# A two-layer hybrid backbone: three weight buffers in the branch merge, and decays beside rates on the two halves of the array

## The chip, the cores and the metric

One core of one Trainium2 chip runs the whole program. The metric is device time in microseconds of one execution; the profile's own span goes from the first to the last instruction.

## The reference

Two layers (DEPTH = 2) over 256 context tokens and 512 latent tokens, D_MODEL = 1024. In each layer a norm, one wide projection, three parallel branches of width 512 (short convolution, bidirectional RWKV-7 scan, neighbourhood attention), the merge of the branches, an output product, and a SwiGLU FFN. The change touches two places. The first is the preparation of the scan's inputs, for two directions:

```python
    for d, offset in enumerate((1, -1)):
        zd = z + mu[d] * (shift_seq(z, offset) - z)
        r, k, v, lw, la = jnp.split(zd, RWKV_SPLITS, axis=-1)
        w_log = -jax.nn.softplus(-(w0[d] + jnp.tanh(lw) @ w2[d])) - 0.5
        decay = jnp.exp(-jnp.exp(w_log.astype(f32)))
        a = jax.nn.sigmoid(a0[d] + la @ a2[d])
```

The second is the merge:

```python
def merge_branches(gate_u, branches, w_up, w_o):
    gates = jax.nn.sigmoid(gate_u.reshape(gate_u.shape[:-1] + (N_BRANCH, D_MODEL)))
    proj = jnp.einsum('btnm,nmd->btnd', jnp.stack(branches, axis=-2), w_up)
    return jnp.sum(gates * proj, axis=-2) @ w_o
```

In the second layer the context tokens are no output, so its merge works on 512 of the 768 tokens.

## The kernel before

Channels lie on partitions and tokens on the free axis, in two segments: s = 0 is the context (256 columns), s = 1 the latent tokens (512 columns). Each large product is split in three: weights and activations are each a rounded part and a rest, and `split_products` (L279 to L281) issues high x high, high x low, low x high. ScalarE rounds a weight slab (ACT), GpSimd subtracts to make its rest (POOL), TensorE multiplies (PE). SyncE issues the loads (SP), in one queue and in program order. Each engine runs its own instructions in order; semaphores (`Count`) join them. The drain that GpSimd makes behind each rest hands the slab's slot back to SyncE.

**Scan stages.** For each of HP = 4 head pairs and each direction d, the weights `SMALL` hold w2 in rows 0 to 63 and a2 in rows 64 to 127, and `LD` holds tanh(lw) and la on the same rows. `decay_and_rate(d)` (L998) makes four plain f32 products: decay ("w") of segment 1 into PSUM bank 7, of segment 0 into bank 6, then rate ("a") the same way. A product waits until ScalarE or VectorE has emptied its bank (`at_bank.free`). ScalarE's sigmoids (L1172) empty them, between two activation table loads (L1163, L1174). There are 16 such groups: 4 in the two prologues ("pro", head pair 0, no scan blocks around them) and 12 in the body stages, where a filler deals these products and the products of the wide projection out between the scan's small block products, in proportion to costs (`COST`, `prep`). The whole order is written out when the kernel is built.

**Merge.** Eight output tiles of 128 channels, two a pass, four passes (the first is written out, the other three are a loop). A pass has six steps, u = 0 to 5: branch n = u % 3 of tile b = u // 3. Each step multiplies one up-weight slab of KM = 4 blocks; its rounded part and rest lie in one of two buffers (`W_HI[u % 2]`, `W_LO[u % 2]`), so ScalarE rounds the slab of step u when the product of step u - 2 is done. The gates of tile b (three branches in one load, L2278) get one sigmoid (L2292), in the loop behind the rounding of that tile's first slab. VectorE multiplies product and gate (L2354), adds (L2360) and splits the sum (L2364, L2366). A product's two banks come round every four steps. SyncE loads the three slabs of a tile and then its gates. Ahead of the first pass GpSimd also loads the residual again (L2329), after the rests of steps 0 and 1.

## Time and profile before

| | us |
|---|---|
| median of 3 runs | 3557.06 (3556.63 to 3567.53) |
| the profiled execution | 3564.53 |
| its span | 3562.8 |

The profile is that of one execution. "Busy" is the time in which an engine has an instruction of the program under way; a figure in brackets behind a timeline row is the engine's idle time just before it, with what ended it. A window row gives its stretch and length, then busy time and records of TensorE's matmuls (PE), its weight loads (PEld), VectorE (DVE), ScalarE (ACT) and GpSimd (POOL), then the granted TensorE clock, the DMA engines' busy share and GB/s. Every plain f32 product leaves two matmul records, every rounded one a single record.

### The profile page before, as it was taken

The numbers are of one execution on the slowest core, as the hardware profiler recorded it, in microseconds if no ns is written. First come the engines' busy times: TensorE is split into PE (matmuls) and PEld (weight loads), VectorE is DVE, ScalarE is ACT, GpSimd is POOL, SyncE is SP. The second block draws the span as 40 slices with busy tenths as digits, with TensorE's granted clock in tenths as the row PEclk, the third lists the DMA queues.
The fourth block names the chain that finished last, engine by engine and source line by source line (L and its number), as shares of the span: only waits on it lengthen the run. The fifth ranks groups of instructions, "written<-read, shape, count | busy, mean of one in ns | idle before, by whom it ended". The sixth has DMA issues, their size and how long they took to land.

```text
span 3562.8 us, 78540 instructions
## 1 busy us (share of the span) xinstructions
PE 3316.8 (93%) x33764; PEld 2601.2 (73%) x33764; DVE 1524.6 (43%) x2844; ACT 1168.5 (33%) x2475; POOL 828.8 (23%) x520
## 2 busy tenths in 40 slices
PE   7999999999999899899999889999999888889998
PEld 5777777777777787688888666676766666658886
DVE  4445454554355652300044464646464455430033
ACT  4333333332333433311111443333432344332222
POOL 2210111110122232222223221111111232324453
PEclk9999999999999999999999999999999999999999
DMA  5423333333355441122111132323133243413322
GB/s 200 135 91 108 106 114 114 93 120 120 101 187 159 150 157 57 42 65 65 60 52 65 71 111 91 101 68 111 57 112 104 88 128 131 144 60 100 94 89 76
DMA packets 246698, 364.84 MB, mean 102 GB/s; under 512 B 154097, under 2 KB 155377, under 8 KB 245889
## 3 DMA queue, kind: packets, MB, share of 16 engines
q1 hardware_dynamic: 226976, 294.57, 27.1%
q10 hardware_dynamic: 14976, 35.66, 2.6%
q0 software_dynamic: 4448, 30.24, 2.4%
q8 instruction: 236, 3.87, 0.5%
q14 instruction: 62, 0.50, 0.0%
HBM read 291.20 MB, written 69.21 MB: 101 GB/s over the span
## 4 chain that ended last, share of the span: by engine, by line
PE 78%; DVE 5%; issue 4%; ACT 4%; DMA 2%; DVEq 2%; POOLq 1%; POOL 1%; PEld 1%; SPq 1%; ACTq 0%; PEldq 0%
PE banks L279 21%; PE banks L280 17%; PE banks L281 17%; PE banks L979 3%; PE banks L1613 3%; PE banks L1600 2%; PE banks L1609 2%; PE banks L1568 1%; PE banks L392 1%; POOLq L2322 1%; PE banks L1622 1%; DMA slot<-in_w_mix 1%; PE banks L1960 1%; DVE arena L595 1%; PE banks L1652 1%
## 5 line engine op out<-in xcount | busy, mean ns | idle before, releaser
L865 POOL TENSOR_TENSOR slot_rounded<-slot,branch_weights_high 128x512 fp32r<-128x512 f32 x188 | 243.9, 1318 | 1429.9 <-ACT branch_weights_high L860 1428.5
L281 PE MATMUL banks<-hx_rounded,slot_rounded 128*128 128x512 f32 (+1 forms) x1624 | 575.7, 355 | 0.0
L279 PE MATMUL banks<-hx_high,weight_parts 128*128 128x512 f32 (+1 forms) x1560 | 556.0, 356 | 18.5 <-DVE hx_low L542 18.0
L280 PE MATMUL banks<-hx_low,weight_parts 128*128 128x512 f32 (+1 forms) x1560 | 555.5, 356 | 0.0
L281 PE MATMUL banks<-hx_high,weight_parts 128*128 128x512 f32 (+1 forms) x1560 | 553.8, 355 | 0.0
L279 PE MATMUL banks<-hx_rounded,branch_weights_high 128*128 128x512 f32 (+1 forms) x1280 | 513.7, 401 | 40.1 <-ACT arena L1172 13.2
L280 PE MATMUL banks<-resid_rounded,branch_weights_high 128*128 128x512 f32 (+1 forms) x1280 | 452.4, 353 | 0.0
L279 PEld LDWEIGHTS banks<-hx_high,weight_parts 128*128 128x128 f32 x1560 | 295.9, 190 | 67.8 <-issue 22.2
L281 PEld LDWEIGHTS banks<-hx_rounded,slot_rounded 128*128 128x128 f32 x1624 | 312.7, 193 | 44.3
L279 PEld LDWEIGHTS banks<-hx_rounded,branch_weights_high 128*128 128x128 f32 x1280 | 245.2, 192 | 119.5 <-issue 60.3
L281 PEld LDWEIGHTS banks<-hx_high,weight_parts 128*128 128x128 f32 x1560 | 295.7, 190 | 42.6
L280 PEld LDWEIGHTS banks<-hx_low,weight_parts 128*128 128x128 f32 x1560 | 296.2, 190 | 40.0
L2576 POOL TENSOR_TENSOR weight_parts<-slot,weight_parts 128x1024 fp32r<-128x1024 f32 x88 | 211.6, 2405 | 467.8 <-ACT weight_parts L2528 467.8
L1152 ACT ACTIVATE arena<-banks 128x512 f32<-128x512 f32 (+1 forms) x144 | 73.9, 513 | 611.5 <-PE banks L281 611.2
L2604 DVE TENSOR_TENSOR arena<-banks,arena 128x256 f32 (+3 forms) x66 | 37.7, 599 | 550.1 <-PE banks L281 550.1
L280 PEld LDWEIGHTS banks<-resid_rounded,branch_weights_high 128*128 128x128 f32 x1280 | 247.4, 193 | 16.7 <-issue 0.5
L1742 DVE TENSOR_TENSOR arena<-arena,banks 128x256 f32<-128x256 f32 (+1 forms) x480 | 172.8, 395 | 197.7 <-PE banks L1613 194.7
L1734 DVE TENSOR_TENSOR arena<-banks,arena 128x128 f32<-128x128 f32 x480 | 119.7, 287 | 150.6 <-PE banks L1600 146.1
L1613 PE MATMUL banks<-arena 64*64 64x64 f32 x3840 | 177.7, 220 | 1.0 <-DVE arena L1734 0.6
L2589 POOL TENSOR_TENSOR weight_parts<-slot,weight_parts 128x1024 fp32r<-128x1024 f32 x42 | 123.4, 2938 | 179.0 <-ACT weight_parts L2551 179.0
L2528 ACT ACTIVATE weight_parts<-slot 128x1024 fp32r<-128x1024 f32 x88 | 93.1, 1058 | 218.2 <-PE banks L281 218.2
L1613 PEld LDWEIGHTS banks<-arena 64*64 64x64 f32 x3840 | 148.4, 135 | 15.8 <-issue 11.4
(247 smaller groups left out, 5836.6 us busy)
## 6 DMA issues: line engine op xcount, KB each, us to landing
slot<-in_w_mix SPq DMA_DIRECT2D x120, 512.0 KB, 4.2
slot<-in_w_ffn_in SPq DMA_DIRECT2D x88, 512.0 KB, 3.5
arena<-chunk_inputs SPq DMA_DIRECT2D x48, 640.0 KB, 4.3
arena<-in_w_ada SPq DMA_DIRECT2D x50, 512.0 KB, 4.4
slot<-in_w_ffn_out SPq DMA_DIRECT2D x44, 512.0 KB, 3.5
slot<-in_w_ada SPq DMA_DIRECT2D x40, 512.0 KB, 3.8
chunk_inputs<-arena SPq DMA_DIRECT2D x80, 256.0 KB, 3.4
arena<-side_projections POOLq DMA_DIRECT2D x16, 1152.0 KB, 6.2
```

The source lines that it names most:

```text
L279: first = nc.tensor.matmul(out, w_hi, x_hi, start=start, stop=False)
L280: nc.tensor.matmul(out, w_hi, x_lo, start=False, stop=False)
L281: return first, nc.tensor.matmul(out, w_lo, x_hi, start=False, stop=stop)
L865: last = nc.gpsimd.tensor_tensor(slots_r[g % 3][:, half], slots[g % 3][:, half], weights_high(g)[:, half], ALU.subtract)
L979: nc.tensor.matmul(pair(6)[s], lhs, rhs, start=True, stop=True).then_inc(done.sem, count)
L1152: nc.scalar.activation(dst, tile_out(l, g, s), ACT.Copy).then_inc(seg_taken[s], 1)
L1613: last = nc.tensor.matmul(A[j][lanes(d), (5 + h) * CHUNK:(6 + h) * CHUNK], T1[j][lanes(d), h], XX[j][lanes(d), X1, h], start=True, stop=True)
L1734: nc.vector.tensor_tensor(T1[j], across(j, 2).rearrange("p (h t) -> p h t", h=2), bc(LEVEL[m - 1], 2), ALU.mult).then_inc(blk_dve[j].sem, 1)
L1742: nc.vector.tensor_tensor(x, x, ps, ALU.add).then_inc(blk_dve[j].sem, 1)
L2528: return nc.scalar.activation(W_HI[u % 2], slots[u][:, :], ACT.Copy).then_inc(f_high.sem, 1)
L2576: nc.gpsimd.tensor_tensor(W_LO[u % 2], slots[u][:, :], W_HI[u % 2], ALU.subtract).then_inc(f_low.sem, 1)
L2589: nc.gpsimd.tensor_tensor(OUT_LO[part(h, m, s)], slots[s][:, :], OUT_HI[part(h, m, s)], ALU.subtract).then_inc(o_low, 1)
```

## The change

Scan stages: the four products of a group come in the order decay and rate of segment 1, then decay and rate of segment 0. The decay uses bank 7 and the rate bank 6 each time, so that the two of a segment stand on different rows of the array and in different banks. Two products make one step of the filler, with the cost of one; the estimate `prep` that spreads the filler goes from 6 to 4. ScalarE's four sigmoids follow the same order.

Merge: the rounded parts and the rests of a slab (512 columns each) go into three buffers, cut out of the same memory; ScalarE rounds the slab of step u when the product of step u - 3 is done. In the loop the gates' sigmoid stands behind the second slab of three instead of the first. In the first pass VectorE makes the rest of step 2, behind its branch rests, and hands back slot 2.

```diff
@@ stage_pe, decay_and_rate
-                for x in range(2):
-                    r = slice(64 * x, 64 * x + 64)
-                    for s in (1, 0):
-                        yield small((("w", "a")[x], d), s, SMALL[r, d * P:(d + 1) * P], LD[r, d, SEGS[s][0]:SEGS[s][1]], pre_prod,
-                                    (pre_act.sem, pre_act.ready(l, hq, 8 * d + 2 * x + 2 - s)))
+                for i, s in enumerate((1, 0)):
+                    for x in range(2):
+                        r, b = slice(64 * x, 64 * x + 64), 1 - x
+                        at_bank.free(b)
+                        nc.tensor.matmul(bank[6 + b][:, 0:SEGS[s][1] - SEGS[s][0]], SMALL[r, d * P:(d + 1) * P], LD[r, d, SEGS[s][0]:SEGS[s][1]],
+                                         start=True, stop=True).then_inc(pre_prod.sem, 1)
+                        at_bank.busy[b] = (pre_act.sem, pre_act.ready(l, hq, 8 * d + 2 * i + x + 1))
+                    mark(("both", s, d))
+                    yield COST[s] * 1.25
...
-            prep, read = 6 * 1.25 * sum(COST) + 2 * 1.25 * out_cost, 3 * 1.25 * out_cost
+            prep, read = 4 * 1.25 * sum(COST) + 2 * 1.25 * out_cost, 3 * 1.25 * out_cost
@@ merge
-        m_prod = Count(sem("merge_products"), KD // 2, NM, primed=2)
+        m_prod = Count(sem("merge_products"), KD // 2, NM, primed=3)
+        m_first = sem("merge_third_rests")
+        def up_weights(parts, u):
+            return parts[u % 3 // 2][:, u % 3 % 2 * KM * P:(u % 3 % 2 + 1) * KM * P]
@@ merge_act
-                act.wait_ge(m_prod.sem, m_prod.ready(l, i, u - 1))
-                nc.scalar.activation(W_HI[u % 2][:, 0:KM * P], slots[u % 3][:, 0:KM * P], ACT.Copy).then_inc(m_high.sem, 1)
+                act.wait_ge(m_prod.sem, m_prod.ready(l, i, u - 2))
+                nc.scalar.activation(up_weights(W_HI, u), slots[u % 3][:, 0:KM * P], ACT.Copy).then_inc(m_high.sem, 1)
...
-                        if u % 3 == 0:
+                        if u % 3 == 1:
                             gates(i + 1, b)
@@ merge_pool
-            for u in range(2, NM):
-                rest(0, u)
+            for u in range(3, NM):
+                rest(0, u, 2 if u == 3 else 1)
@@ merge_dve
+            dve.wait_ge(att_spilled[0].sem, att_spilled[0].ready(l, att_spilled[0].passes - 1, 16))
+            dve.wait_ge(m_high.sem, m_high.ready(l, 0, 3))
+            nc.vector.tensor_tensor(up_weights(W_LO, 2), slots[2][:, 0:KM * P], up_weights(W_HI, 2), ALU.subtract).then_inc(m_first, 1)
+            dve.drain().then_inc(slab_used[2], 1)
```

The order of TensorE's instructions before, in the first body stage of layer 0, forward direction (L979 with `banks<-arena` are the decay and rate products, the 64x64 rows are scan block products):

```order
L281 MATMUL banks<-hx_rounded,slot_rounded 128x256
L979 MATMUL banks<-arena 128x512
L1600 MATMUL banks<-arena 64x64 x8
L979 MATMUL banks<-arena 128x256
L1609 MATMUL banks<-arena 64x64 x4
L1613 MATMUL banks<-arena 64x64 x4
L1609 MATMUL banks<-arena 64x64 x4
L1613 MATMUL banks<-arena 64x64 x4
L979 MATMUL banks<-arena 128x512
L979 MATMUL banks<-arena 128x256
L1600 MATMUL banks<-arena 64x64 x8
L279 MATMUL banks<-hx_rounded,branch_weights_high 128x512
```

And of the changed kernel at the same place (L1007 is the new line of these products, and block lines stand 4 higher):

```order
L281 MATMUL banks<-hx_rounded,slot_rounded 128x256
L1604 MATMUL banks<-arena 64x64 x8
L1007 MATMUL banks<-arena 128x512 x2
L1007 MATMUL banks<-arena 128x256 x2
L1613 MATMUL banks<-arena 64x64 x4
L1617 MATMUL banks<-arena 64x64 x4
L1613 MATMUL banks<-arena 64x64 x4
L1617 MATMUL banks<-arena 64x64 x4
```

Four products with block work between them became two pairs next to each other, and nothing is left between the first pair and the second.

The order of ScalarE's instructions before, in the merge's loop of layer 0 (L2288 rounds a slab, L2292 is the gates' sigmoid):

```order
L2288 ACTIVATE weight_parts<-slot 128x512
...
L2292 ACTIVATE arena<-arena 128x2304
...
L2288 ACTIVATE weight_parts<-slot 128x512
...
L2288 ACTIVATE weight_parts<-slot 128x512
...
L2288 ACTIVATE weight_parts<-slot 128x512
L2292 ACTIVATE arena<-arena 128x2304
...
L2288 ACTIVATE weight_parts<-slot 128x512
...
L2288 ACTIVATE weight_parts<-slot 128x512
```

And of the changed kernel (L2301 and L2305):

```order
L2301 ACTIVATE weight_parts<-slot 128x512
...
L2301 ACTIVATE weight_parts<-slot 128x512
...
L2305 ACTIVATE arena<-arena 128x2304
...
L2301 ACTIVATE weight_parts<-slot 128x512
...
L2301 ACTIVATE weight_parts<-slot 128x512
...
L2301 ACTIVATE weight_parts<-slot 128x512
L2305 ACTIVATE arena<-arena 128x2304
...
L2301 ACTIVATE weight_parts<-slot 128x512
```

Each sigmoid moved behind one more rounding.

The order of GpSimd's instructions before, in the merge's opening of layer 1 (L2321 makes rests, L2329 loads the residual; the last row is written out for steps 2 to 5):

```order
L2182 TENSOR_TENSOR arena<-arena 128x256 x6
L865 TENSOR_TENSOR slot_rounded<-slot,weight_parts 128x512 x4
L2321 TENSOR_TENSOR weight_parts<-slot,weight_parts 128x512 x2
L2329 DMA resid<-residual_kept 128x6144
L2321 TENSOR_TENSOR weight_parts<-slot,weight_parts 128x512 x4
```

And of the changed kernel on GpSimd (L2334, L2342), then on VectorE (L2252 branch rests, L2359 the moved rest):

```order
L2186 TENSOR_TENSOR arena<-arena 128x256 x6
L865 TENSOR_TENSOR slot_rounded<-slot,weight_parts 128x512 x4
L2334 TENSOR_TENSOR weight_parts<-slot,weight_parts 128x512 x2
L2342 DMA resid<-residual_kept 128x6144
L2334 TENSOR_TENSOR weight_parts<-slot,weight_parts 128x512 x3
```

```order
L2166 COPY arena<-banks 128x8x16
L2252 TENSOR_TENSOR branches_low<-arena,branches_high 128x512 x4
L2166 COPY arena<-banks 128x8x16
L2252 TENSOR_TENSOR branches_low<-arena,branches_high 128x512 x8
L2359 TENSOR_TENSOR weight_parts<-slot,weight_parts 128x512
```

One rest left GpSimd behind the residual's load and stands on VectorE behind the eight branch rests.

## Rows read from the trace of the kernel before

**Rows 1.** The page: span of the profiled execution.
```profile
span 3562.8 us, 78540 instructions
```

**Rows 2.** Busy time by stretch: busy us and records of each engine, granted clock.
```profile
84.00:1000.00 916.00, 872.61 (x13002) 668.41 (x13005) 436.15 (x1005) 309.74 (x860) 122.06 (x100) 0.98 0.37 111
1225.70:1339.40 113.70, 105.28 (x577) 91.18 (x577) 68.58 (x100) 38.49 (x41) 34.95 (x26) 0.96 0.53 179
1257.20:1273.90 16.70, 16.70 (x98) 14.74 (x97) 10.94 (x16) 4.55 (x5) 5.65 (x4) 1.00 0.54 180
3008.00:3103.70 95.70, 78.47 (x289) 61.07 (x289) 50.49 (x62) 32.28 (x40) 33.94 (x25) 0.88 0.52 177
3099.70:3102.40 2.70, 2.70 (x13) 2.03 (x11) 1.38 (x2) 1.06 (x1) 1.35 (x1) 1.00 0.74 272
```

**Rows 3.** Timeline of TensorE in the merge, idle time in brackets.
```profile
1244.23 0.55 PE L279 MATMUL banks<-branches_high,weight_parts 128*128 128x256 f32 x1 [4.48 <-POOL weight_parts L2321]
...
3023.95 0.77 PE L279 MATMUL banks<-branches_high,weight_parts 128*128 128x512 f32 x1 [4.88 <-POOL weight_parts L2321]
3024.52 0.63 PE L280 MATMUL banks<-branches_low,weight_parts 128*128 128x512 f32 x1
...
3053.25 0.49 PE L279 MATMUL banks<-branches_high,weight_parts 128*128 128x512 f32 x1 [3.91 <-POOL weight_parts L2321]
```

**Rows 4.** Timeline of GpSimd when the residual comes back, and its DMA.
```profile
1242.71 1.26 POOL L2321 TENSOR_TENSOR weight_parts<-slot,weight_parts 128x512 fp32r<-128x512 f32 x1 [9.16 <-issue]
...
3011.27 0.58 POOL L2329 DMA_DIRECT2D resid<-residual_kept  x1 [0.62 <-issue]
...
3022.43 1.26 POOL L2321 TENSOR_TENSOR weight_parts<-slot,weight_parts 128x512 fp32r<-128x512 f32 x1 [6.87 <-issue]
...
resid<-residual_kept POOLq DMA_DIRECT2D x1, 3072.0 KB, 11.0
```

**Rows 5.** Timeline of VectorE at the merge's opening, layer 0.
```profile
1226.01 9.23 DVE L2242 TENSOR_TENSOR branches_low<-arena,branches_high 128x768 fp32r<-128x768 f32 x8 [0.61 <-issue]
```

**Rows 6.** Timeline of SyncE and ScalarE, layer 1 second pass; later gate loads.
```profile
3043.43 0.63 SPq L2278 DMA_DIRECT2D arena<-gate_projections  x1
...
3049.77 1.48 ACT L2292 ACTIVATE arena<-arena 128x1536 f32<-128x1536 f32 x1 [5.20 <-DMA arena<-gate_projections]
3051.16 1.13 ACT L2288 ACTIVATE weight_parts<-slot 128x512 fp32r<-128x512 f32 x2
...
arena<-gate_projections SPq DMA_DIRECT2D x4, 768.0 KB, 4.7
```

**Rows 7.** TensorE groups by form, and one attention stretch of the timeline.
```profile
L979 PE MATMUL banks<-arena 64*128 64x512 f32 x64 | 38.0, 675 | 14.0 <-ACT arena L1172 9.5 <-ACT arena L1152 4.5
L979 PE MATMUL banks<-arena 64*128 64x256 f32 x64 | 22.3, 430 | 0.7 <-ACT arena L1152 0.7
...
1206.96 0.70 PE L1947 MATMUL banks<-arena 64*128 64x256 f32 x4
```

**Rows 8.** Timeline, prologue of layer 0, reverse direction.
```profile
122.73 1.55 PE L979 MATMUL banks<-arena 64*128 64x512 f32 x4
...
124.53 1.05 ACT L1172 ACTIVATE arena<-banks,vec 128x512 f32<-128x512 f32 x2
125.27 2.24 PE L979 MATMUL banks<-arena 64*128 64x512 f32 x4 [0.99 <-ACT arena L1172]
...
128.44 0.77 PE L279 MATMUL banks<-hx_rounded,branch_weights_high 128*128 128x512 f32 x1 [0.93 <-ACT arena L1172]
```

**Rows 9.** Timeline of TensorE, first body stage of layer 0, both directions.
```profile
219.82 1.12 PE L979 MATMUL banks<-arena 64*128 64x512 f32 x2
...
222.81 1.55 PE L979 MATMUL banks<-arena 64*128 64x512 f32 x4
...
308.24 1.55 PE L979 MATMUL banks<-arena 64*128 64x512 f32 x4 [0.84 <-ACT arena L1172]
...
311.09 0.55 PE L279 MATMUL banks<-hx_rounded,branch_weights_high 128*128 128x256 f32 x1 [1.30 <-ACT arena L1172]
```

More of the change, by code:

```diff
@@ L1161, in preparation @@
                     k = 8 * d
-                    yield at(("w", d)) - 1
+                    yield at(("both", 1, d)) - 1
                     act.preload_act_table_set(SIGMOID)
-                    for x, dst, bias in ((0, TMP[3], V_W0), (1, TMP[5], V_A0)):
-                        yield at((("w", "a")[x], d))
-                        if d == 1:
-                            act.wait_ge(*((pre_dve.sem, pre_dve.ready(l, hq, 5)) if x == 0 else (stored[4].sem, stored[4].ready(l, hq, 32))))
-                        elif st == BODY:
-                            act.wait_ge(*((post_dve.sem, post_dve.free(l, hp, 4)) if x == 0 else (stored[4].sem, stored[4].ready(l, hp, 64))))
-                        act.wait_ge(pre_prod.sem, pre_prod.ready(l, hq, k + 2 * x + 2))
-                        for s in (1, 0):
-                            nc.scalar.activation(dst[:, TSEG[s][0]:TSEG[s][1]], pair(6)[s], ACT.Sigmoid, bias=vec[:, bass.ds(hq + (bias + d * HP), 1)])\
-                              .then_inc(pre_act.sem, 1)
+                    for i, s in enumerate((1, 0)):
+                        yield at(("both", s, d))
+                        for x, dst, bias in ((0, TMP[3], V_W0), (1, TMP[5], V_A0)):
+                            if d == 1 and i == 0:
+                                act.wait_ge(*((pre_dve.sem, pre_dve.ready(l, hq, 5)) if x == 0 else (stored[4].sem, stored[4].ready(l, hq, 32))))
+                            elif st == BODY and i == 0:
+                                act.wait_ge(*((post_dve.sem, post_dve.free(l, hp, 4)) if x == 0 else (stored[4].sem, stored[4].ready(l, hp, 64))))
+                            act.wait_ge(pre_prod.sem, pre_prod.ready(l, hq, k + 2 * i + x + 1))
+                            nc.scalar.activation(dst[:, TSEG[s][0]:TSEG[s][1]], bank[7 - x][:, 0:SEGS[s][1] - SEGS[s][0]], ACT.Sigmoid,
+                                                 bias=vec[:, bass.ds(hq + (bias + d * HP), 1)]).then_inc(pre_act.sem, 1)
                     act.preload_act_table_set(LOGEXP)
@@ L1176, in preparation @@
                     nc.scalar.activation(TMP[6], TMP[7], ACT.Square).then_inc(pre_act.sem, 1)
-                    yield max(at(("a", d)) + 4, at(("norm", d)) - 1)
+                    yield max(at(("both", 0, d)) + 4, at(("norm", d)) - 1)
                     act.wait_ge(pre_dve.sem, pre_dve.ready(l, hq, k + 2))
@@ L1290, in preparation @@
                         mixed(2, d, TMP[2]).then_inc(made.sem, 1)
-                    g = max(g + 1, at(("a", d)) + 1)
+                    g = max(g + 1, at(("both", 0, d)) + 1)
                     yield g
-                    dve.wait_ge(pre_act.sem, pre_act.ready(l, hq, k + 2))
+                    dve.wait_ge(pre_act.sem, pre_act.ready(l, hq, k + 3))
                     for (t0, t1), (c0, c1) in zip(TSEG, SEGS):
@@ L2255, in six @@
                     pe.wait_ge(br_low, 3 * HP * l + HP * (n + 1))
-                    pe.wait_ge(m_low.sem, m_low.ready(l, i, u + 1))
+                    if opening and u == 2:
+                        pe.wait_ge(m_first, l + 1)
+                    else:
+                        pe.wait_ge(m_low.sem, m_low.ready(l, i, u + 1))
                     if u >= 4:
@@ L2265, in six @@
                             w = slice(k * P, (k + 1) * P)
-                            _, last = split_products(pair(2 * (u % 4))[s], W_HI[u % 2][:, w], W_LO[u % 2][:, w], BR_HI[:, n, k, c0:c1], BR_LO[:, n, k, c0:c1],
+                            _, last = split_products(pair(2 * (u % 4))[s], up_weights(W_HI, u)[:, w], up_weights(W_LO, u)[:, w], BR_HI[:, n, k, c0:c1], BR_LO[:, n, k, c0:c1],
                                                      k == 0, k == KM - 1)
@@ L2314, in merge_act, with rest @@
                         weights(i + 1, u)
[L2315 removed]
+                        if u % 3 == 1:
                             gates(i + 1, b)
         def merge_pool(pool, l):
[L2319 removed]
+            def rest(i, u, count=1):
                 pool.wait_ge(m_high.sem, m_high.ready(l, i, u + 1))
[L2321 removed]
+                nc.gpsimd.tensor_tensor(up_weights(W_LO, u), slots[u % 3][:, 0:KM * P], up_weights(W_HI, u), ALU.subtract).then_inc(m_low.sem, count)
                 pool.drain().then_inc(slab_used[u % 3], 1)
```

4 lines of the change are left out of this document (1 added, 3 removed).

## The prediction

> **What bounds the kernel now.** I read the windows first. In the scan stages of layer 0 TensorE is busy for 872.6 of 916 us at a granted clock of 0.98 [rows 2]. So time taken off TensorE's queue there should come off the end, if nothing takes its place. The two merges are different: 113.7 and 95.7 us long, with granted clocks of 0.96 and 0.88 [rows 2]. Two stretches without a wait give the price of a step: four steps of layer 0 take 16.7 us, 4.18 each, and one of layer 1 takes 2.72 (the window's 2.70 and its edges) [rows 2]. At 24 steps the merges need 100.3 and 65.3 us. They lose 13.4 and 30.4 us, 43.8 in all, to waits of TensorE and to the low clock behind them.
>
> The timeline says where. The fourth step (u = 3) of the first pass waits 4.48 us in layer 0 and 4.88 in layer 1 for GpSimd's rest, and a wait of 3.91 comes back in the loop of layer 1 [rows 3]. After the 4.88 the matmuls of 512 columns start 0.43 us apart (3024.52 is one of them), which is 1.2 GHz; in the 2.72 us step, 12 matmuls, they start 0.23 apart, 2.4 GHz [rows 2, 3]. So a wait costs more than its length: the step behind it has some eight slow matmuls, 1.6 us.
>
> Two causes. First, GpSimd starts its rest of step 3 only at 3022.43, after 6.87 us that the profile calls issue. It issued the residual's load at 3011.27, and that load takes 11.0 us to land: 3022.3 [rows 4]. So the drain behind the rest of step 2 waits for the load's landing. Layer 0 shows the same 9.16 us [rows 4]. Second, in the loop ScalarE stands 5.20 us before the gates' sigmoid, for their load, and the roundings that follow in its queue wait with it (3051.16, straight behind the sigmoid) [rows 6].
>
> **The merge, part by part.**
>
> *The opening.* Step 2's rest moves to VectorE, behind eight branch rests. In layer 0 these end at 1226.01 + 9.23 = 1235.2 [rows 5]. A rest of 512 columns costs some 0.7 us there (two thirds of 9.23 / 8, less overlap; no row shows it), so step 2 starts near 1236.0, about 0.7 late; I charge that. In layer 1 product 2 is not due before VectorE is done, so it is free. GpSimd goes on to the rest of step 3, which signals before its drain. So the drain that waits for the residual now delays step 4 and not step 3. Two products more are done by then. In layer 1 step 4 is due at about 3021.6 (step 0 starts with the window at 3008.0 and at the low clock takes twice 2.72; then three steps of 2.72). Its rest can start at 3022.43 at the earliest. The gates of tile 1 are now loaded at the same time, 1 MB with the slab, so residual and gates land later than each would alone: I add 0 to 2.5 us, take 1.4, and the rest is ready at 3025.1. The wait is 3.5 and the low clock behind it 1.6. In layer 0 I find step 4 due at 1236.0 + 8.4 = 1244.4. The gates, issued near 1236.5, need 6.3 us as in [rows 6], then a sigmoid of half as many columns more (2.1), a rounding and a rest: 1246.8, and 1247.5 with the shared DMA. The wait is 3.0 and the clock about 1.3.
>
> *The loop.* With three buffers a rounding is free one product sooner, and the sigmoid has two roundings ahead of it. What is late next? There is a ring: gates land, sigmoid 1.5, rounding 0.6, rest 1.3, drain and slab issue 0.5, next gates' load. The load lands 6.3 us after issue at 3043.43, 4.7 in the median of the later ones [rows 6]. Half a pass is then 8.6 us against three products at 8.2. The opening leaves 2 to 3 us of slack, and six half passes eat 0.4 each, so at 4.7 the ring almost never shows. At 6.3 it costs 2.0 a half pass, 12 less the slack: 10 us. I take 2. Layer 0's three products last 12.5 us, and its ring (load 6.3, sigmoid 2.1, the rest 2.4) 10.8: no wait.
>
> *The sum.* Left in layer 0: slow first product 1.5, step 2 0.7, step 4 4.3, entry into the output product 0.5, together 7 of 13.4: gain 6.4. Left in layer 1: slow start 3, step 4 5.1, ring 2, entry 1, together 11 of 30.4: gain 19.3. The merge gives **25**, with bounds 15 (ring at 6.3, nothing else) and 30.
>
> **Decay and rate, part by part.** The 128 records (two for each f32 product) are busy 38.0 + 22.3 = 60.3 us [rows 7]. If the halves ran side by side everywhere, 30 would go; that is the upper bound on work. Do they? No decay product runs beside a rate now. The nearest row is attention's: four records on 64 rows, 256 columns, are over in 0.70 us. Here one such product, two records, takes 22.3 / 32 = 0.70 us alone [rows 7]. So different row halves do overlap. But the second half must find its bank empty when the first does, and that I go through by kind of group:
>
> - Prologue, 4 groups. From first product to next tile 128.44 - 122.73 = 5.7 us [rows 8]. Bank 6 still holds the last tile, so the first two products run one behind the other, 1.9. The table load holds the first sigmoid until 124.53 as now; two sigmoids follow, of 0.69 and 0.6. The second pair ends near 126.4, and the next tile, on bank 7, starts at 126.6: gain 1.8, twice this where both banks are free. I take 2 each, 8.
> - Body of layer 0, forward, 3 groups. There is no idle time before [rows 9], because block products stand between. Now the second pair stands right behind the first and waits for both sigmoids, about 1.3 us and some bank wait. The 1.5 saved in products is spent: 0.
> - Body of layer 0, reverse, 3 groups. The waits of 0.84 and 1.30 [rows 9] become one of 1.05, and one 512 and one 256 product (1.55) go. Gain 2.6 each, 8.
> - Body of layer 1, 6 groups, whose order is between these two: 1.5 each, 9.
>
> That is 25. TensorE is not the end of every stretch: 43 of 916 us are idle for other reasons [rows 2], and in the prologues the first block also waits for its stored inputs. I count four fifths: **20**, with bounds 5 (halves one behind the other, only waits gained) and 30. ScalarE's and VectorE's work is the same in number and size; the cost of the new `prep` estimate, a shift of filler by under 3%, is nothing in the sum and 3 us either way in the range.
>
> Here the Trainium skill speaks against me. "TensorEngine Tiling (Array Packing)", section Performance Considerations, says that tiling speeds TensorE up but not the emptying of PSUM, which may become the bottleneck; by that rule every group would stay as long as its four sigmoids, and this part would give its lower bound, 5. The 0.84 and 1.30 us waits of [rows 9] agree with it in adjacent groups, and it is rival 1 below.
>
> **The time.** 25 + 20 = 45 us. The profiled execution took 3564.5 with a span of 3562.8 [rows 1]; it would take 3519.5. It lies 7.5 above the median of the runs shown, so I predict 3557.1 - 45 = 3512.
>
> **The rivals.**
>
> 1. *Emptying of banks sets the groups.* For it: the waits just named. Against it: in reverse body groups block work stands between the pairs and covers the sigmoids. Left are the waits: the 0.84 gone and 0.25 off the 1.30 in the 3 reverse groups (3.3), some 0.4 in each prologue group (1.7), nothing elsewhere. That is 5 in place of 20: 3527. Chance 0.15.
> 2. *The gates' load sets the loop.* The merges would draw data faster than now (177 GB/s in layer 1 [rows 2]), and every load would take the 6.3 us of the slow one: 10 in place of 2, and the opening 2 worse: 35 gained, 3522. Chance 0.15.
> 3. *No measurable change.* Steps 2 and 4 wait as long as step 3 did, the loop's wait only moves to step 5, and the pairs run in turn: 5 and 3 gained, 3549. It needs both parts to fail. Chance 0.05.
> 4. *Slower.* One mechanism: ScalarE takes decay and rate sigmoids in one stretch, and the block copies queued behind them hold the scan's chain in the 12 body groups. It has to cost 45 / 12 = 3.8 us a group beyond the sums above to cancel the gain; a pair (1.05) and two sigmoids (1.3) make 2.4. Slower begins beyond 4.6. At 5 it gives 3572. Chance 0.02.
> 5. *Both parts at their better bounds*, 30 and 30: 3497. Chance 0.05.
>
> My forecast has 0.58 and its own range is 3504 to 3520. The range 3499 to 3532 leaves out rivals 3 and 4, a part of 1 and of 5. A run tells 0.3%, 10.7 us, from no change: faster 0.93, same 0.05, slower 0.02.
>
> **What would show it.** The merge windows should be about 107 and 76 us. TensorE's wait at step 3 of the first pass should be gone, and one of 2 to 5 us should stand at step 4, behind GpSimd's rest. In layer 1's loop no wait above 1.5 us should be left. VectorE's moved rest should take about 0.7 us. Of the decay and rate records, pairs should start within 0.02 us of each other in the body groups and not in the prologues; their waits for L1172's successor should sum to no more than the 9.5 us of now [rows 7]. I am wrong if scan stages keep their length while the products overlap, or if waits of over 2 us come back at step 2 or 5 of the loop.

## The result and the profile after

The changed kernel takes 3535.76 us (median of 4 runs, 3534.99 to 3538.69), the kernel before 3559.52 (4 runs, 3556.63 to 3567.53): a ratio of 0.9926, 95% interval 0.9911 to 0.9942. It is faster, by 24 us in the medians and 29 between the profiled executions; the profiled execution of the kernel before is 5 us above its median, so what follows is split up from 29. The prediction said 45 and a range that ended at 3532.

The page's first line, to be read beside [rows 1]:

```profile
span 3533.6 us, 78544 instructions
```

Windows of the changed kernel over the scan of layer 0 and the two merges, columns as in [rows 2]:

```profile
84.00:998.00 914.00, 866.04 (x13018) 666.04 (x13016) 437.69 (x1005) 311.09 (x860) 125.53 (x102) 0.99 0.36 112
1223.90:1334.50 110.60, 106.11 (x576) 92.88 (x576) 67.83 (x100) 38.06 (x41) 32.40 (x25) 0.94 0.53 184
2995.70:3074.00 78.30, 71.42 (x288) 57.69 (x288) 50.48 (x62) 31.56 (x40) 32.55 (x24) 0.90 0.62 211
```

TensorE's own stretches are a little shorter than the windows: from the first merge product's start to the last one's end the merges went from 113.2 to 110.4 us and from 94.5 to 78.1. That is 19.2 of the 29. In the scan of layer 0 TensorE has 6.6 us less to do in 914 us than it had in 916, yet the stretch is hardly shorter.

The timeline of TensorE in the merge, answering [rows 3]:

```profile
1247.89 0.55 PE L279 MATMUL banks<-branches_high,weight_parts 128*128 128x256 f32 x1 [4.32 <-issue]
...
3016.02 0.76 PE L279 MATMUL banks<-branches_high,weight_parts 128*128 128x512 f32 x1 [6.51 <-issue]
3016.59 0.63 PE L280 MATMUL banks<-branches_low,weight_parts 128*128 128x512 f32 x1
```

Step 3 waits for nothing now; step 4 waits 4.32 and 6.51 us, and starts at the slow clock (0.57 us from one 512-column product to the next here). In the loop no wait is left, where [rows 3] had 3.91. GpSimd, ScalarE and SyncE around it, layer 1:

```profile
2999.04 0.58 POOL L2342 DMA_DIRECT2D resid<-residual_kept  x1 [0.62 <-issue]
...
3014.66 1.27 POOL L2334 TENSOR_TENSOR weight_parts<-slot,weight_parts 128x512 fp32r<-128x512 f32 x1 [11.25 <-ACT weight_parts L2301]
...
3002.42 0.44 SPq L2291 DMA_DIRECT2D arena<-gate_projections  x1
...
3012.58 1.48 ACT L2305 ACTIVATE arena<-arena 128x1536 f32<-128x1536 f32 x1 [9.24 <-DMA arena<-gate_projections]
3013.97 1.65 ACT L2301 ACTIVATE weight_parts<-slot 128x512 fp32r<-128x512 f32 x3
```

and for the gates' load that SyncE issues at 3002.42:

```profile
DMA to landing us min/median/max: 10.1/10.1/10.1
```

GpSimd's rest no longer stands behind "issue", its drain, as in [rows 4], but behind ScalarE's rounding, and this one behind the sigmoid of tile 1's gates, whose load took 10.1 us. In layer 0 the same load took 9.2.

TensorE in the first body stage of layer 0 (answers to [rows 9]), only what waits and the pairs:

```profile
216.35 1.27 PE L1007 MATMUL banks<-arena 64*128 64x512 f32 x4
218.50 1.27 PE L1007 MATMUL banks<-arena 64*128 64x256 f32 x4 [0.88 <-ACT arena L1176]
...
237.29 0.70 PE L1580 MATMUL banks<-arena 64*64 64x128 f32 x8 [2.64 <-ACT arena L1703]
...
304.43 1.13 PE L1007 MATMUL banks<-arena 64*128 64x512 f32 x4 [0.75 <-ACT arena L1156]
...
308.62 0.70 PE L1007 MATMUL banks<-arena 64*128 64x256 f32 x4
...
310.34 0.36 PE L279 MATMUL banks<-hx_rounded,branch_weights_high 128*128 128x256 f32 x1 [1.02 <-ACT arena L1176]
```

The reverse pairs run side by side: four records of 512 columns in 1.13 us where two took 1.12 [rows 9]. The forward group's second pair waits 0.88 us for a sigmoid and runs in turn, 1.27 us. The wait of 2.64 us for ScalarE's block copy is new. It stands once in each body stage of layer 0, and ScalarE's timeline says what the copy stood behind:

```profile
232.28 0.60 ACT L1156 ACTIVATE arena<-banks 128x512 f32<-128x512 f32 x1 [1.56 <-PE banks L281]
232.78 1.05 ACT L860 ACTIVATE branch_weights_high<-slot 128x1024 fp32r<-128x1024 f32 x1
233.73 0.83 ACT L1183 ACTIVATE arena<-arena 128x769 f32<-128x769 f32 x1
234.46 0.83 ACT L1184 ACTIVATE arena<-arena 128x769 f32<-128x769 f32 x1
235.36 0.85 ACT L1186 ACTIVATE arena<-arena 128x769 f32<-128x769 f32 x1
236.29 0.32 ACT L1190 ACTIVATE arena<-arena 128x4 f32<-128x4 f32 x2
236.51 0.50 ACT L1699 ACTIVATE arena<-banks,arena 128x64 f32<-128x64 f32 x2
236.90 0.34 ACT L1703 ACTIVATE arena<-banks 128x64 f32<-128x64 f32 x2
```

The exponentials of the decays (L1183 to L1190) come between the block's two state copies; in the kernel before they came after the next block's first copies. Nobody moved them by hand. The places between the scan's block steps where the filler may put products are numbered; they are called gaps here. The exponentials stand one gap ahead of the key norm's mark, and with pairs charged as one product the norm of the forward half is dealt out in gap 14 and not 15.

The scan by stages, each from the first product of one scan block (L1568 before, L1572 after) to that six blocks on, in us; "prologue" is the start of block 0. The labels are those of the next section:

```
kernel          prologue   body stages of layer 0         body stages of layer 1
before          168.7      208.7 207.6 206.2  sum 622.6   174.4 174.8 173.7  sum 523.0
after           164.8      209.3 208.2 205.4      622.8   173.6 172.4 172.6      518.6
m_only          169.2      208.7 207.6 206.3      622.5   174.2 174.3 173.9      522.4
p_only          165.6      209.3 208.1 205.5      622.9   172.3 172.0 170.3      514.6
p_prep6         167.2      209.2 205.3 207.9      622.4   174.2 174.6 175.8      524.7
prep4           168.1      210.0 212.9 216.7      639.5   183.0 179.4 184.0      546.4
exp_place       166.5      205.7 205.7 203.7      615.1   173.4 171.8 172.3      517.5
g_last          166.9      209.4 205.9 206.4      621.7   172.8 172.3 170.6      515.7
r_late          165.3      205.9 206.6 208.8      621.4   173.0 172.5 172.0      517.5
resid_pieces    163.3      209.3 205.5 207.6      622.4   173.3 172.2 171.2      516.6
adjacent        165.6      208.5 206.3 204.9      619.7   178.1 177.9 177.6      533.6
charge2         164.0      202.6 201.2 201.2      605.0   175.3 176.9 175.1      527.3
mixed           165.2      202.6 201.2 201.2      605.0   173.2 172.4 172.6      518.1
mixed_all       163.1      202.6 201.2 201.2      605.0   172.2 172.3 171.1      515.6
```

The table also shows how far one profile can be trusted. The kernels after, p_only, g_last, r_late and resid_pieces have the same scan in both layers. Their prologues spread over 3.6 us, their layer 0 sums over 1.5, and their layer 1 sums over 4.0.

### The profile page after: what moved, and what is told of

The parts are those of the page before. It is cut to its first block, busy times and chain, and to the rows that moved or that the text cites. A ratio compares the mean times of both kernels' runs of the same rounds, so it can differ in the third digit from the quotient of the medians.

```text
span 3533.6 us, 78544 instructions
## 1 busy us (share of the span) xinstructions
PE 3301.4 (93%) x33764; PEld 2597.5 (74%) x33764; DVE 1526.1 (43%) x2846; ACT 1170.0 (33%) x2475; POOL 827.3 (23%) x518
## 3 DMA queue, kind: packets, MB, share of 16 engines
q1 hardware_dynamic: 226976, 294.57, 27.1%
## 4 chain that ended last, share of the span: by engine, by line
PE 78%; DVE 7%; ACT 4%; issue 4%; DVEq 2%; DMA 2%; POOLq 1%; PEld 1%; POOL 1%; SPq 0%; ACTq 0%; PEldq 0%
PE banks L279 21%; PE banks L280 18%; PE banks L281 18%; PE banks L1617 3%; PE banks L1604 2%; PE banks L1613 2%; PE banks L979 1%; PE banks L392 1%; PE banks L1626 1%; PE banks L1572 1%; PE banks L1007 1%; PE banks L1964 1%; POOLq L2335 1%; DVE arena L595 1%; DMA slot<-in_w_mix 1%
```

## The experiments

Ratios are to the kernel before, on the same chip, with 95% intervals. The chips differ from experiment to experiment, and the median of the kernel before was 3559.5 to 3567.5 us on them; so two versions measured on different chips are compared by their ratios or by their traces, not by their times.

**The two parts alone.** m_only is the kernel before with the hunks of the merge, p_only the one with those of decay and rate.

> The kernel before with the merge part of the change alone (three buffers, gates' sigmoid behind the second slab, VectorE's rest of step 2). The trace of the changed kernel has the two merges 19.2 us shorter, the prediction's sum had 25. If the parts add up, this kernel is 19 us faster than the one before in its span, with merge windows near 110.4 and 78.1 us and a wait at step 4 of 4 and 6.5 us. If the scan part's loss comes from the merge's side (it shares no tile with it, so I give this little), more than 24 us are gained here.

> The kernel before with the decay and rate part alone, the new prep estimate with it. Theory 1, the prediction's sum: 20 us faster. Theory 2, read from the changed kernel's trace (prologues 4 and 3.5 us shorter, the body stages of layer 0 together 1.6 longer, those of layer 1 4.6 shorter): 10 us faster. A new wait of 2.5 to 3.3 us for ScalarE's block copy should stand in the body stages of layer 0.

m_only: 0.9943 (0.9928 to 0.9957), 3543.1 us; span 3538.3. Its merges take 108.8 and 77.5 us, 21.4 less than before, and its scan is that of before to 0.6 us. Its waits at step 4 are 3.98 and 5.55. p_only: 0.9959 (0.9945 to 0.9972), 3552.5 us, span 12.1 below. The scan part alone gives some 12 where 20 were forecast, and nothing in layer 0's body stages (622.9 against 622.6). The two ratios together take off 0.98%, both parts in one kernel 0.74% (0.58 to 0.89). The intervals leave room for a plain sum, but the runs do not show one: in the traces the parts give 24.5 and 12.1, and together 29.2.

**The estimate.** p_prep6 is p_only with

```diff
-            prep, read = 4 * 1.25 * sum(COST) + 2 * 1.25 * out_cost, 3 * 1.25 * out_cost
+            prep, read = 6 * 1.25 * sum(COST) + 2 * 1.25 * out_cost, 3 * 1.25 * out_cost
```

and prep4 is the kernel before with this line turned the other way.

> The decay and rate part alone, but with the old estimate prep of six units, so that the pacing of tile work among the scan's blocks is nearly that of before. Theory A: the gain lost in the body stages of layer 0 is due to the pacing that the new estimate shifted (less tile work dealt out before each gap); then the body stages of layer 0 get shorter by up to the predicted 8 us against before, and the kernel is 15 to 20 us faster than before. Theory B: it is lost because ScalarE takes four sigmoids in one stretch and block copies stand behind them; then the new 3 us wait for the block copy stays, the body stages of layer 0 are within 2 us of before, and the gain stays at 10. Since the filler's yields are now fewer and larger, pacing can differ a little under either.

> The kernel before with nothing changed but the estimate prep, 6 to 4, so that only the dealing out of tile work among the gaps moves, with the decay and rate products still one after the other and charged at their old cost. Theory A (the pacing costs): slower than before by 3 to 10 us, in the body stages of layer 0 above all. Theory B (the sigmoids in one stretch cost): within 2 us of before.

p_prep6: 0.9963 (0.9950 to 0.9977), 3551.8 us. The wait for L1703 is still there, 7.9 us in layer 0's scan, and another, of L1634 for ScalarE's L1688, has come (10.3). The three signs of theory B are all there: the wait stays, layer 0's body is within 0.2 us of before, and the gain stays where it was. But the run could not tell the theories apart. The old estimate did not bring back the old pacing, since the pairs are still charged half: the forward norm of layer 0 stays in gap 14, and its reverse norm goes from 51 to 49. prep4: 1.0100 (1.0081 to 1.0118), 3604.8 us, 39 slower. I had expected 3 to 10. The body stages are 16.9 and 23.4 us longer. Part of that is a wait for the blocks' inputs, which this row gives for layer 0:

```profile
PE banks L1568 <- DMA arena<-chunk_inputs: 5.6, 3, 2.2
```

That is 5.6 of the 16.9; that it comes from tile work left to the end of a stage is argued, and the rest was not worked out. A change of one constant that adds no instruction is worth more than the whole change. My "nothing in the sum and 3 us either way" for it was a guess with no row behind it.

**Where the exponentials stand.** exp_place is the changed kernel with

```diff
-                    yield max(at(("both", 0, d)) + 4, at(("norm", d)) - 1)
+                    yield max(at(("both", 0, d)) + 4, at(("norm", d)) - (0 if l == 0 and st == BODY and d == 0 else 1))
```

> The changed kernel with one thing moved: in the forward preparation of layer 0's body stages ScalarE's five exponentials and small copies of the decays stand one gap later, behind the state copies of the scan's block and not between its two halves, where they stood before the change. Theory A: this order, shifted by the new pacing, and not the four sigmoids in one stretch, makes TensorE wait 2.6 to 3.3 us for the block copy; then the wait goes, and the three body stages of layer 0 get 2 to 3 us shorter each, 6 to 9 in all against the changed kernel. Theory B: TensorE's time is set by something later in the scan's chain, or the copies wait for the sigmoids anyway; then the wait moves and less than 2 us are gained.

0.9881 (0.9865 to 0.9898), 3525.4 us. The waits of 2.64 us for L1703 are gone in all three stages (1.8 and 0.6 us of it come back in later blocks), and the stages are 3.6, 2.5 and 1.7 us shorter than in the changed kernel, 7.7 in all: theory A, with a rest. The span falls by 5.9 only, since step 4 of layer 1's merge waits 8.75 us here and not 6.51; why is open. VectorE, which needs those exponentials, is late instead:

```profile
240.94 0.36 PE L279 MATMUL banks<-hx_rounded,branch_weights_high 128*128 128x256 f32 x1 [2.30 <-DVE arena L1321]
```

So one thread put back leaves the others where the charges moved them.

**The step 4 of the merge's opening.** g_last and r_late are the changed kernel with

```diff
             weights(0, 3)
             gates(0, 0)
-            gates(0, 1)
             weights(0, 4)
             weights(0, 5)
+            gates(0, 1)
```

and with GpSimd's residual load behind `rest(0, 5)`. place_g_last has exp_place's edit and g_last's.

> The changed kernel with ScalarE's second gates' sigmoid of the opening placed behind the roundings of steps 4 and 5, not before them. Theory A: step 4 of the first pass waits for the landing of tile 1's gates (9.3 and 10.2 us after issue, beside the residual's load), through sigmoid, rounding and rest; then the waits of 4.3 and 6.5 us become 0 in layer 0 and about 2 in layer 1 (the residual lands only then and GpSimd's drain waits for it), and the merges lose 5 to 6 us each, the low clock with them: 9 to 12 us in all. Theory B: GpSimd's drain behind the residual's load is the later one, as the prediction had it; then the waits stay within 1 us and nothing is gained.

> The changed kernel with the residual's load (and the next layer's table) issued behind GpSimd's last rest of the first pass and not before its rest of step 3. Theory A (gates' landing sets step 4, and shares its time with the residual's load): the gates land 5.9 us after issue, as they did alone in the kernel before, and not 9.3 and 10.2; the waits at step 4 shrink by 3.4 and 4.3 us to about 1 and 2. Theory B (the drain behind the residual sets step 4): the waits go to below 1 as well, with the gates' time unchanged. The time to landing tells them apart. The residual's load now falls into the loop, where it may delay slabs or gates by some us: total gain 3 to 10.

> Both edits on the changed kernel: exponentials one gap later in layer 0's forward preparation, second gates' sigmoid of the opening behind two roundings. They share no stage, so the gains should add up: 15 to 20 us below the changed kernel if theory A holds for both, 40 to 45 below the kernel before.

g_last: 0.9870 (0.9850 to 0.9890), 3520.6 us; merges 103.2 and 74.3 us, 11.0 less than in the changed kernel. Behind its first product layer 0's merge has no wait at all, layer 1's has 3.38, and that one is GpSimd's drain. The residual's load, issued at 2987.9, lands 12.2 us later, at 3000.1, and the next rest starts right behind it:

```profile
3000.35 1.27 POOL L2334 TENSOR_TENSOR weight_parts<-slot,weight_parts 128x512 fp32r<-128x512 f32 x1 [8.05 <-issue]
```

Theory A. place_g_last: 0.9846 (0.9831 to 0.9861), 3511.7 us; the gains add up in the spans, 5.9 and 14.8 singly and 20.8 together. r_late: 0.9908 (0.9893 to 0.9923), 3535.8 us. The waits at step 4 fall to 2.50 and 2.08, and the two gates' loads in this stretch of layer 1 land early:

```profile
DMA to landing us min/median/max: 4.5/4.6/4.7
```

That is theory A's sign. But the residual's load now meets the loop, which has waits of 4.60 and 5.31 for GpSimd's rests. The span is that of the changed kernel to 0.2 us, and the two intervals of the ratios overlap: no gain is shown, against the 3 to 10 expected.

**The residual in pieces.** resid_pieces takes the residual's load from GpSimd and has SyncE issue it in seven pieces:

```diff
                         load_gates(sp, l, i, b)
+                        if i or b:
+                            r = 2 * i + b - 1
+                            r = slice(r * T, (r + 1) * T) if r < KD - 2 else slice(r * T, KD * T)
+                            sp.dma_start(resid[:, r], (a["resid_dram"] if l else a["x"])[:, r]).then_inc(resid_back, 16)
```

> The changed kernel with the residual's load taken from GpSimd's queue and issued by SyncE in seven pieces, one behind each gates' load of the merge. Neither GpSimd's drain nor tile 1's gates meet the whole load now. If the shared DMA makes the gates late, they land 5 to 7 us after issue rather than 9.3 and 10.2, and the waits at step 4 fall to 1 to 2.5 us; the pieces lengthen the later gates' loads by at most 1 us each, which the loop's slack takes. 6 to 9 us gained. If the loop of layer 1 has no slack, waits come back in it (prediction's ring), and nothing or less is gained.

0.9876 (0.9861 to 0.9891), 3518.5 us. The waits at step 4 are 2.47 and 2.39, the loop has one of 1.06, the merges take 105.3 and 72.0 us: 11.2 less than in the changed kernel, more than expected. The waits are 6.0 us shorter together and one is new (1.06), so some 6 of the 11.2 are slow clock that no longer follows them: the granted clock of the two merges is 0.98, where it was 0.94 and 0.90.

**The old charges.** charge2 is the changed kernel with prep at six units and

```diff
-                    yield COST[s] * 1.25
+                    yield COST[s] * 2.5
```

which puts every tile, norm and sum into the gap of before. adjacent charges the same, but all of it behind the second pair, so that no block product comes between the pairs: `yield 0 if s else 2.5 * sum(COST)`. mixed has charge2's numbers in layer 0 and the change's in layer 1. charge2_g_last adds g_last's edit; all3 adds the pieces too.

> The changed kernel with each pair of decay and rate products charged at its old cost (two products) and prep at six units, so that every tile, norm and sum stands at the gap where it stood before the change; the two pairs of layer 0's forward groups fall into different gaps, with block products between them. Theory A: the loss in layer 0's body stages came from the places that the new charges moved (the exponentials and VectorE's work with them), one place having its turn after another when a single one is put back; then no wait of over 2 us stands in these stages, each gets 3 to 5 us shorter than in the changed kernel, the body stages of layer 1 as much as before or 1 better, 10 to 15 us in all. Theory B: TensorE's saved time cannot be had there, since the chain of the scan's blocks sets the length; then the stages stay within 1 us of the kernel before, and 2 to 3 us are gained on the changed kernel.

> The same charges and, in the opening of the merge, the second gates' sigmoid behind the roundings of steps 4 and 5, which was worth 7 and 4 us in the two layers. The gains should add up: 20 to 27 us below the changed kernel under theory A of the run with the charges alone, 13 under theory B.

> Old charges, second gates' sigmoid behind the roundings, and the residual in seven pieces by SyncE, all on the changed kernel. With the sigmoid moved, layer 0 has no wait left at step 4 and layer 1 has 3.4 us, for GpSimd's drain behind the residual; the pieces should take these away and the slow clock behind them: 4 to 6 us beyond the kernel with charges and sigmoid alone, unless the loop waits for its data.

> As the run with the old charges (each tile, norm and sum at the gap of before), but with the second pair of decay and rate products right behind the first in every group, so that no block product stands between them. Theory A1: what the old charges brought in layer 0's body stages (17.6 us against the kernel before) came from the exponentials and the other threads standing where they stood; then the stages keep 15 us or more of it. Theory A2: it came from the block products between the two pairs, which cover ScalarE's first two sigmoids; then the forward groups wait 0.9 us again and run in turn (2 us a stage), and the stages keep 11 to 12 us. Layer 1's body stages are 1 to 2 us longer each than before with the old charges, with a wait of 2 us for ScalarE behind the second pair; if that pair's late gap makes it, it goes here and layer 1 comes out 1 to 2 us shorter a stage.

> The changed kernel with the old charges in layer 0 alone; layer 1 keeps the new ones. Theory: what matters is where each layer's sequence happens to put ScalarE's and VectorE's work between the scan's block steps, each layer apart; then layer 0's body stages are 17 to 18 us shorter than before, those of layer 1 4 to 6 us shorter, and the kernel is 17 to 20 us faster than the changed one. Rival: layer 1's stages depend on what clock or phase they are entered with; then they do not come out at 172 to 173.5 us each.

> Charges by layer, second gates' sigmoid behind the roundings, the residual in seven pieces by SyncE. The kernel with all three and the old charges in both layers stood at 3506 us; layer 1's body stages should take 5 to 7 us off that: 3499 to 3501 on the scale of that run, 60 us below the kernel before.

charge2: 0.9896 (0.9881 to 0.9911), 3525.4 us. Layer 0's body stages are 17.6 us shorter than before (theory A, and more than it said); layer 1's are 4.3 longer (2.6 in charge2_g_last and all3, which have the same scan), which neither theory had. adjacent: 0.9951 (0.9936 to 0.9965), 3544.9 us; layer 0 keeps 2.9 of the 17.6. Every tile, norm and sum stands in the gap of before in both kernels, so theory A1 is out. What is left is theory A2's cause, the missing block products, but not its account: the price is 14.7 and not 6, the wait is 0.29 us in the forward groups and 0.83 in the reverse ones, and layer 1 gets worse still, its waits for L1688 (7.0 us in all) nearly as before (8.1). The difference can be read in one reverse group. TensorE in adjacent:

```profile
300.13 1.13 PE L1007 MATMUL banks<-arena 64*128 64x512 f32 x4 [0.75 <-ACT arena L1156]
302.09 1.80 PE L1007 MATMUL banks<-arena 64*128 64x256 f32 x4 [0.83 <-ACT arena L1176]
```

and the ten microseconds around it, in adjacent, and in charge2, where one block step stands between the pairs:

```profile
300.00:310.00 10.00, 9.04 (x101) 6.68 (x103) 1.46 (x4) 7.83 (x20) 2.48 (x2) 0.66 0.01 2
```

```profile
297.00:307.00 10.00, 8.98 (x177) 7.14 (x178) 5.66 (x12) 7.82 (x21) 2.50 (x2) 1.00 0.23 69
```

TensorE is busy equally long, but at a granted clock of 0.66 it gets through 101 matmuls and not 177. In the second and third stage of adjacent the same two waits are followed by 0.83 and 1.00. The kernel before has the same dip behind its waits of 0.84 and 1.30:

```profile
310.00:320.00 10.00, 8.91 (x108) 7.98 (x109) 4.14 (x9) 3.80 (x7) 0.00 (x0) 0.66 0.44 122
```

Over the 20 us from a reverse group's first product on, the granted clock is 0.83, 0.83 and 0.91 in the three stages of before, 0.83, 0.91 and 1.00 in adjacent, and 1.00 three times in charge2. By my estimate (what is missing to 1, times 20 us) that is 8.6 us of the 17.6 in the kernel before, and 5.2 of the 14.7 in adjacent. The rest of the 17.6 is 4.0 us of idle time (30.3 to 26.3) and 5 us of products.

In charge2's forward groups the pairs fall into gaps 6 and 8, with block products between:

```profile
215.13 1.67 PE L1007 MATMUL banks<-arena 64*128 64x512 f32 x4
216.73 0.46 PE L1604 MATMUL banks<-arena 64*64 64x64 f32 x16
217.49 0.34 PE L1613 MATMUL banks<-arena 64*64 64x64 f32 x8 [0.30 <-DVE arena L1738]
...
218.33 0.70 PE L1007 MATMUL banks<-arena 64*128 64x256 f32 x4
```

Four records of 256 columns take 0.70 us here; in the changed kernel, behind a wait of 0.88, they ran one behind the other, 1.27. In layer 1 the late second pair puts ScalarE's table load and square in front of a block copy, and TensorE waits 2.04 for it:

```profile
2166.98 1.28 ACT L1178 ACT_TABLE_LOAD   x1
2168.27 0.84 ACT L1180 ACTIVATE arena<-arena 128x769 f32<-128x769 f32 x1
2169.03 0.26 ACT L1688 ACTIVATE arena<-banks 128x128 f32<-128x128 f32 x1
```

```profile
2169.34 0.34 PE L1634 MATMUL banks<-arena 64*64 64x64 f32 x8 [2.04 <-ACT arena L1688]
```

mixed: 0.9861 (0.9845 to 0.9878), 3512.5 us; its stages are those of charge2 in layer 0 and those of the change in layer 1, as the theory had it. charge2_g_last: 0.9856 (0.9841 to 0.9872), 3509.5 us, 27.1 below the changed kernel in the spans, where 20 to 27 were expected. all3: 0.9838 (0.9825 to 0.9852), 3506.0 us, 3.5 beyond charge2_g_last on the same chip, where 4 to 6 were expected. **mixed_all, the best version, takes 3497.6 us (5 runs, 3492.2 to 3498.8): 0.9817 (0.9801 to 0.9833).** That is 67 us below the kernel before on its chip, against 60 expected. Its merges:

```profile
1201.60:1305.00 103.40, 103.32 (x576) 90.80 (x576) 69.02 (x99) 38.50 (x40) 31.73 (x24) 0.97 0.56 196
2962.70:3029.80 67.10, 66.97 (x288) 54.89 (x288) 45.90 (x62) 31.44 (x39) 31.71 (x23) 0.98 0.71 245
```

TensorE is busy for all but 0.2 us of both, 3.1 and 1.8 us above the 100.3 and 65.3 that the prediction worked out as the need of 24 steps.

## Why the prediction was wrong

It was right that the kernel gets faster and by which two routes, and wrong in the size: 24 us in the medians and 29 in the spans where 45 stood. The step that failed is the sentence that sets the new pacing at nothing; it cost the 8 us of layer 0's body. The opening's step 4 in the merge was mis-sized by some 6 us besides. By its own terms:

**The merge, 25: measured 19.2.** Loop and step 2 came out better than charged. The ring never shows (0, charged 2): layer 1's later gates land in 4.3 to 5.8 us, near the 4.7 of [rows 6], and rival 2 is out. Step 2 costs nothing (charged 0.7), though VectorE's rest there takes 1.78 us, not 0.7. The opening's step 4 came out worse: waits of 4.32 and 6.51 where 3.0 and 3.5 stood, and 2.7 and 2.6 us of slow clock behind them (the step takes 7.06 and 5.46 us against 4.34 and 2.88) where 1.3 and 1.6 stood. The first product of layer 0 takes 6.91 us and not 4.18, 2.7 more where 1.5 stood. The step at fault is "residual and gates land later than each would alone: I add 0 to 2.5 us, take 1.4". Beside a load of 3 MB the gates' 768 KB took 10.1 us; r_late has the same load at 4.7 when the residual comes later. So the gates' sigmoid, and not the drain behind the residual that the prediction took for the last to end in layer 1, sets step 4. The drain comes next, as g_last shows. Left above the need: 10.1 us in layer 0 (7 predicted) and 12.8 in layer 1 (11).

**Decay and rate, 20 (four fifths of 25): measured about 10, and 12 in p_only.**
- *Prologues, 8.* Layer 0 gave 3.9, and 1.8 to 5.4 over the five kernels with this scan. Layer 1 gave 2.9 in p_only, whose merge is built as before (from layer 0's last block to layer 1's first 1221.6 to 1218.7). This term held as far as such a spread can tell.
- *Body of layer 0, 8.* Measured nothing: 0.2 us longer, and the tail behind it 1.3. Here the prediction failed, in the sentence that sets "the cost of the new `prep` estimate" at nothing; the halved charge of a pair, the other half of the new pacing, has no term at all, and p_prep6 shows that the old estimate without the old charge brings nothing back. The new charges move the forward norm by one gap and ScalarE's exponentials with it, into the scan's chain: 2.64 us of wait in each stage, and in two stages of three 2 to 3.5 us of slow clock on top. That the pairs themselves are worth more than was forecast is what charge2 shows: 17.6 and not 8. Of the some 6 us of its first stage 5.3 come in the reverse group and 0.9 in the forward one, forecast 2.6 and 0. The term for the reverse group counted two waits and 1.55 us of products; it left out the slow clock that stood behind those waits (0.83, 0.83 and 0.91 over 20 us, above), as the prediction itself had counted it in the merge. Without these 8.6 us the 17.6 would be 9, close to the 8 of the sum.
- *Body of layer 1, 9.* Measured 4.4 in the changed kernel, but 8.4 in p_only, 7.3 in g_last, 5.5 in r_late and 6.4 in resid_pieces, with the same scan. So this term fell short by something between 1 and 5 us, and which is open. The same charges move things there too; why this placement is a good one and charge2's a poor one was seen for one wait (2.04) and not worked out for the rest.

**The rivals.** The time lies between rival 1 and rival 3, and neither is what happened. Rival 1, emptying of banks: waits for L1172's successor sum to 7.9 us, within the 9.5 that was promised. Where nothing stands between the pairs they do wait for sigmoids: 0.88 in the changed kernel's forward groups, 0.83 in the reverse groups of adjacent. With one block step between them that wait is gone, and the gain of the overlap is there. The Trainium skill's "TensorEngine Tiling (Array Packing)", section Performance Considerations, says that tiling speeds up TensorE but not the emptying of PSUM. The waits of 0.88 and 0.83 agree with it. Rival 4 named the right victim, ScalarE's block copies held up and the scan's chain behind them, and the wrong cause: the four sigmoids in one stretch. exp_place leaves the sigmoids as they are, and its wait for the copy is gone. Its price, 2.64 plus the clock, was under the point from which it makes the kernel slower. In layer 1 of charge2 a copy does stand behind the sigmoids' table load and a square (2.04), so that mechanism exists; the changed kernel's loss is another.

**The checks.** Merge windows 110.4 and 78.1 (promised 107 and 76); step 3's wait gone; at step 4 one of 4.32 in layer 0, within the promised 2 to 5, and one of 6.51 in layer 1, above them; no loop wait above 0.2. In layer 0 pairs do start together in the reverse body groups and not in the prologue, but in the forward body groups the second pair runs in turn; in layer 1's prologue the first pair does start together, against the forecast. And the prediction's own sign of being wrong, scan stages that keep their length while the products overlap, came true in layer 0's body.

## What to carry to other kernels

Where a work list is paced by estimated costs, an edit of the estimates is an edit of the order on every engine: list what changes its slot, and look for engine work that lands between two links of a dependent chain, before costing it at nothing. When an edit makes one item cheaper, try it first with the old charge, so that the item alone is measured. And a load's landing time read beside idle queues is no price for the same load beside a large one; ask what else is in flight in the slot to which it moves.

## What the runs showed of the hardware

- **The same wait costs different amounts by its clock.** The wait of 2.64 us stands in three stages of five kernels whose layer 0 scan is the same (after, p_only, g_last, r_late, resid_pieces). Over the 15 us that follow, the granted clock was 1.00 in five of the 15, 0.89 in two, 0.77 in three and 0.67 or 0.68 in five; so the first stage takes 205.9 us in r_late and 209.3 in the changed kernel. For it, the changed kernel and r_late between 235 and 250 us:

```profile
235.00:250.00 15.00, 12.10 (x141) 9.47 (x142) 5.96 (x14) 6.05 (x20) 1.41 (x2) 0.66 0.22 80
```

```profile
235.00:250.00 15.00, 11.18 (x193) 8.71 (x185) 7.65 (x17) 6.91 (x22) 1.93 (x2) 1.00 0.35 110
```

  What decides which it is was not found. A difference of 3.4 us between two versions of such a stage is no evidence of a change without the clock beside it.
- **Two short waits can bring the slow clock as well as a long one.** 0.75 and 0.83 us, 1.1 us apart, in adjacent: 0.66, 0.83 and 1.00 over the next 10 us in the three stages. In charge2, 0.75 and later 1.02, with block products between: 1.00 in all three.
- **Sharing the DMA.** Layer 1's 768 KB of gates land in 4.2 to 6.3 us in the kernel before, and in 10.1 beside the residual's 3 MB in the changed one. Issued in seven pieces between the gates' loads, the residual costs the loop of layer 1 one wait of 1.06 us in resid_pieces and none in mixed_all.
